# A two-layer decoder trunk on one core: masked decays, paired squares, block steps in a triangular inverse, queries spread by DMA, and four reorderings

## What is computed

```
# gated delta, per head, in chunks of c tokens
decay  = exp(where(causal, b[:, None] - b[None, :], -inf))
attn   = (q @ k.T) * decay
a      = strict_lower((k_beta @ k.T) * decay)
sol    = triangular_solve(I + a, [v * beta, k_beta * exp(b)])
o      = rms_norm(o_delta, norm_w) * silu(z)          # root mean square over 256 values of a head
# cross-attention of the samples, per sample and head
s      = q_sample @ mem_k.T * HD_X ** -0.5            # 256 memory rows, 256 values per head
# merge
merged = g0 * (o_ret @ w_ret) + g1 * (o_gdn @ w_gdn) + g2 * (o_mem @ w_mem)
```

## Time and profile before

| what | value |
|---|---|
| median of 3 runs | 1855.25 us (1853.64 to 1856.99) |
| the profiled execution, its own time | 1852.71 us |
| its span, first to last instruction | 1850.9 us |
| mean granted TensorE clock | 0.999 |
| busy: PE, DVE, ACT, POOL | 1803.7, 1321.4, 890.8, 118.8 us |
| DMA | 368.20 MB, mean 199 GB/s |

### The profile page before, as it was taken

The page is one execution under the profiler, slowest core; times in us unless marked ns, Lnnn a source line. Parts: engine busy times, 40 slices in busy tenths (PEclk is TensorE's granted clock), DMA queues, the critical chain, the costliest instruction groups (busy, mean ns, idle before and its releaser), DMA issues.

```text
span 1850.9 us, 40385 instructions
## 1 busy us (share of the span) xinstructions
PE 1803.7 (97%) x16247; PEld 1744.1 (94%) x16247; DVE 1321.4 (71%) x2077; ACT 890.8 (48%) x1044; POOL 118.8 (6%) x174
## 2 busy tenths in 40 slices
PE   6999999999999999999999999999999899999998
PEld 6999999988988999999999999998889799989998
DVE  6677577787777867777567765768777776877764
ACT  5443364546574254543364434454566434354433
POOL 0000001111210100000000000010112010000000
PEclk9999999999999999999999999999999999999999
DMA  7776667766864656666667766676778465556654
GB/s 232 218 207 191 180 198 225 235 227 211 284 227 137 198 160 226 170 191 168 173 200 219 206 185 201 195 243 206 236 242 267 144 201 171 169 148 186 182 164 133
DMA packets 433619, 368.20 MB, mean 199 GB/s; under 512 B 9395, under 2 KB 411125, under 8 KB 432811
## 3 DMA queue, kind: packets, MB, share of 16 engines
q1 hardware_dynamic: 409560, 276.60, 50.2%
q0 software_dynamic: 23872, 89.03, 14.3%
HBM read 338.90 MB, written 26.69 MB: 198 GB/s over the span
## 4 chain that ended last, share of the span: by engine, by line
PE 76%; DVE 14%; issue 5%; ACT 2%; DMA 2%; DVEq 0%; SPq 0%; ACTq 0%
PE proj L687 49%; PE proj L710 4%; PE proj L705 4%; PE proj L706 4%; DVE wl L1870 3%; PE proj L661 2%; PE aux L752 1%; PE aux L922 1%; ACT wh L1371 1%; PE aux L1144 1%; DMA raw<-w_mem_v 1%; PE aux L867 1%; PE aux L883 1%; DMA raw<-w_branch_gdn 1%; PE aux L1017 1%
## 5 line engine op out<-in xcount | busy, mean ns | idle before, releaser
L1870 DVE TENSOR_TENSOR wl<-raw,wh 128x2048 fp32r<-128x2048 f32 (+1 forms) x280 | 599.2, 2140 | 196.4 <-ACT wh L1371 172.6
L1371 ACT CAST wh<-raw 128x2048 fp32r<-128x2048 f32 (+1 forms) x280 | 500.3, 1787 | 245.0 <-PE proj L687 94.2
L687 PE MATMUL proj<-xh,wh 128*128 128x264 f32 x2624 | 379.6, 287 | 2.2 <-issue 2.2
L687 PE MATMUL proj<-xl,wh 128*128 128x264 f32 x2624 | 380.6, 285 | 0.0
L687 PE MATMUL proj<-xh,wl 128*128 128x264 f32 x2624 | 370.9, 284 | 0.1
L687 PEld LDWEIGHTS proj<-xl,wh 128*128 128x128 f32 x2624 | 341.3, 188 | 12.5 <-issue 12.3
L687 PEld LDWEIGHTS proj<-xh,wh 128*128 128x128 f32 x2624 | 340.1, 188 | 4.8 <-issue 3.0
L687 PEld LDWEIGHTS proj<-xh,wl 128*128 128x128 f32 x2624 | 338.9, 188 | 0.7 <-DVE wl L1870 0.6
L706 PE MATMUL proj<-hl,wh 128*128 128x264 f32 x704 | 173.3, 283 | 0.0
L705 PE MATMUL proj<-hh,wh 128*128 128x264 f32 x704 | 173.0, 283 | 0.0
L1392 ACT ACTIVATE gate<-gate 128x264 f32<-128x264 f32 x88 | 37.4, 425 | 242.1 <-DVEq L1905 242.0
(11 more groups left out here) (472 smaller groups left out, 2235.4 us busy)
## 6 DMA issues: line engine op xcount, KB each, us to landing
raw<-ffn_w_in SPq DMA_DIRECT2D x176, 512.0 KB, 5.2
raw<-w_in SPq DMA_DIRECT2D x80, 1024.0 KB, 5.6
raw<-ffn_w_out SPq DMA_DIRECT2D x64, 704.0 KB, 4.6
sring<-cache_mem_k POOLq DMA_DIRECT2D x32, 512.0 KB, 4.9
sring<-cache_mem_v POOLq DMA_DIRECT2D x32, 512.0 KB, 3.9
out<-sring POOLq DMA_DIRECT2D x32, 512.0 KB, 4.5
sring<-state_gdn POOLq DMA_DIRECT2D x30, 512.0 KB, 4.9
raw<-w_mem_v SPq DMA_DIRECT2D x8, 1024.0 KB, 6.2
```

Source lines behind the costliest of these rows:

```text
L687: mm = pe.matmul(o, w[:, s, k * 256 + t * P:k * 256 + (t + 1) * P], a[:, k, :], **go)
L1371: act.copy(wh[:, slot, 0:size], raw[:, slot, 0:size]).then_inc(hi_done[slot], 1)
L1870: dve.tensor_sub(wl[:, slot, 0:size], raw[:, slot, 0:size], wh[:, slot, 0:size].bitcast(F32)).then_inc(split_done[slot], 1)
```

## The change

Values that are computed stay the same. Seven edits:

1. The future half of a decay is set by the minimum: in place of 0 the minimum is taken with `future`, 0 in the triangle and -10000 outside, so both multiplications by `tri` go, and L2437 takes the decay itself as its last factor; L2441 and L2416 go.
2. DVE adds the squares of the two halves of a head (`pair_sums(sqd)`, in gz after the remainder of group 2), and `gm` has four products in place of eight.
3. The levels of groups 4 and 5 of the inverse work on blocks with tile positions: 16 and 24 products of 32 x 32 x 32 (`pair_blocks`, `pair_corrections`), then 8 and 8 of 64 x 64 x 64 (`half_blocks`, `half_corrections`). `gw`, `c_t` and `t_m` go. The second half of the last `gu` of the small levels moves from the end of group 3 into group 4.
4. Queries: DVE copies the row in float32 to `qrow`, POOL stores it to a tensor in DRAM, waits for the landing, and loads two rows at a time to all 128 partitions (`spread`, 256 KB, three buffers `qsp`). PE's `spread` goes. Of the 16 scores a layer, three stand in mq, where five stood.
5. `smt` moves one sixth of a group later; `rkn` is turned three products later, and DVE's `kn` is made in conv tile 1 of group 0, ahead of the remainder for group 2, where it stood in group 1. `mpt0` starts at bank 2.
6. `gdt` goes to bank 2 and `gkS` to bank 1; in x0 group 0 DVE stacks the keys (releases `gkS`) ahead of `sample_outputs`.
7. At the end of rg `gated(1)`, `gated_low` and `tell("o_ret")` stand ahead of `query_part(1)` and of the remainder.

```diff
-QUERIES = ["mkt0", "mqs0", "mkt1", "sp0", "gaw", "mqs1", "sp1", "gab", "sp2", "mqs2", "sp3", "sp4"]
+QUERIES = ["mkt0", "mqs0", "mkt1", "gaw", "mqs1", "gab", "mqs2"]
 STEPS = (["n1", "q1", "p1", "n2", "q2"] + QUERIES
-         + ["mqs3", "sp5", "ms0", "sp6", "ms1", "sp7", "mpt0", "sp8", "sp9", "mpt1", "sp10", "sp11",
-            "mo0", "sp12", "sp13", "mo1", "sp14", "sp15", "smt", "spt"]
+         + ["mqs3", "ms0", "ms1", "mpt0", "mpt1", "mo0", "mo1", "smt", "spt"]
...
+FIRST_BANK = {**{f"{n}{g}": b for g in range(LEVELS) for n, b in (("gc", 3), ("gu", 0))}, "gdt": 2, "gkS": 1, "mpt0": 2, "smt": 0, "gkn": 1, "gus": 1, "gmt": 3,
...
+        future = masks[:, 4, :]
...
+            def store_query(l, h):
+
+                pool.wait_ge(M["mqs"], l * H + h + 1)
+                passed(pool)
+                pool.dma_start(queries[l, h], qrow[:, h % 2, :]).then_inc(query_stored, 16)
+                pool.wait_ge(query_stored, 16 * (l * H + h + 1))
+
+            def spread(l, n):
+
+                h, b = n // 4, 2 * (n % 4)
+                if n >= 3:
+                    pool.wait_ge(unit_used[(n - 3) % SRING], l * (NUNIT // SRING) + (n - 3) // SRING + 2)
+                passed(pool)
+                pool.dma_start(qsp[n % 3][:], queries[l, h, b:b + 2].rearrange("b d -> (b d)").partition_broadcast(P)).then_inc(unit_loaded[n % SRING], 16)
...
+                store_query(l, 0)
+                for n in range(3):
+                    spread(l, n)
...
-                for n in range(SRING, V_UNIT):
-                    unit(l, n)
+                for n in range(2 * NS):
+                    if n in (0, 1, 3):
+                        store_query(l, (n + 1) // 2 + 1)
+                    if n + SRING < V_UNIT:
+                        unit(l, n + SRING)
+                    if n + 3 < 2 * NS:
+                        spread(l, n + 3)
...
-                def spread(n):
-
-                    h, b = n // 4, 2 * (n % 4)
-                    if b == 0:
-                        pe.wait_ge(M["mqs"], l * H + h + 1)
-                    o = begin(l, f"sp{n}")
-                    for z in range(2):
-                        mm = pe.matmul(o[:, 0, z * 256:(z + 1) * 256], selr[0:ROWS, b + z:b + z + 1].broadcast_to([ROWS, P]),
-                                       qst[:, h * 256:(h + 1) * 256], start=True, stop=True)
-                    end(mm, f"sp{n}")
-
...
+                def rest_inner(g, t, k):
+
+                    if g == 2 and (t, k) == (1, 1):
                         ready("sall")
                         turn(l, "smt", [(m * P, sall[:, m, :]) for m in range(2)])
-                    else:
-                        ready("spr")
-                        turn(l, "spt", [(m * 32, ps[:, m * P:(m + 1) * P]) for m in range(2)])
-
-                def rest(g):
-                    if g < 2:
-                        spread(13 + 2 * g)
-                products(l, "rv", xh, xl, after=rest, mid=rest_middle)
+
+                products(l, "rv", xh, xl, mid=rest_middle, inner=rest_inner)
...
+                    if g == 1 and (t, k) == (1, 0):
+                        ready("rot")
+                        turn(l, "rkn", [((2 * h + t) * P, rot[:, 4 + h, t * P:(t + 1) * P]) for h in range(H) for t in range(2)])
...
+                def pair_blocks(o):
+
+                    for n in range(8):
+                        for i in (0, 2 * BLK):
+                            first, second = slice(i, i + BLK), slice(i + BLK, i + 2 * BLK)
+                            mm = pe.matmul(o[second, n * BLK:(n + 1) * BLK], a_t[n // 4][first, n % 4, second], blk_t[first, 1, n, :],
+                                           start=True, stop=True, tile_position=(i, i + BLK))
+                    return mm
+
+                def pair_corrections(o):
+
+                    for n in range(8):
+                        c = slice(n * BLK, (n + 1) * BLK)
+                        for i in (0, 2 * BLK):
+                            second = slice(i + BLK, i + 2 * BLK)
+                            pe.matmul(o[i:i + BLK, c], blk_y[second, n, :], blk_t[second, 0, n, :], start=True, stop=True, tile_position=(i + BLK, i))
+                        mm = pe.matmul(o[BLK:2 * BLK, c], blk_t[BLK:2 * BLK, 0, n, :], blk_y[BLK:2 * BLK, n, :],
+                                       start=True, stop=True, tile_position=(BLK, BLK))
+                    return mm
+
+                def half_blocks(o):
+
+                    for n in range(8):
+                        mm = pe.matmul(o[HALF_P:P, n * HALF_P:(n + 1) * HALF_P], a_t[n // 4][0:HALF_P, n % 4, HALF_P:P], t_h[0:HALF_P, n, :],
+                                       start=True, stop=True, tile_position=(0, HALF_P))
+                    return mm
+
+                def half_corrections(o):
+
+                    for n in range(8):
+                        mm = pe.matmul(o[0:HALF_P, n * HALF_P:(n + 1) * HALF_P], y_h[HALF_P:P, n, :], t_t[n // 4][HALF_P:P, n % 4, HALF_P:P],
+                                       start=True, stop=True, tile_position=(HALF_P, 0))
+                    return mm
...
                     if g < SMALL and (t, k) == (1, 4):
                         corrections(g, 0)
-                    elif 0 < g < SMALL and (t, k) == (0, 1):
+                    elif 0 < g <= SMALL and (t, k) == (0, 1):
                         corrections(g - 1, 1)
-                    if g == SMALL + 1 and t == 0 and k in (4, 6):
-                        s = (k - 4) // 2
-                        pe.wait_ge(inv_t, l * 9 + 7 + s + 1)
-                        turn(l, f"gw{s}", [(q * P, t_t[s][:, q, :]) for q in range(4)])
+                    elif g == SMALL and (t, k) == (1, 4):
+                        pe.wait_ge(inv_y, l * 6 + 5)
+                        o = begin(l, f"gu{g}")
+                        end(pair_corrections(o[:, 0, :]), f"gu{g}")
+                    elif g == SMALL + 1 and (t, k) == (1, 4):
+                        pe.wait_ge(inv_y, l * 6 + 6)
+                        pe.wait_ge(inv_t, l * 8 + 7)
+                        o = begin(l, f"gu{g}")
+                        end(half_corrections(o[:, 0, :]), f"gu{g}")
...
-                        for s in range(2):
-                            if g > SMALL:
-                                pe.wait_ge(inv_m, l * 2 + s + 1)
-                            else:
-                                pe.wait_ge(inv_t, l * 9 + 5 + s + 1)
-                            o = begin(l, f"gy{g}{s}")
-                            for q in range(4):
-                                mm = pe.matmul(o[:, 0, q * P:(q + 1) * P], c_t[s][:, q, :], t_m[s][:, q, :], start=True, stop=True)
-                            end(mm, f"gy{g}{s}")
+                        pe.wait_ge(inv_t, l * 8 + g + 1)
+                        o = begin(l, f"gc{g}")
+                        end(pair_blocks(o[:, 0, :]) if g == SMALL else half_blocks(o[:, 0, :]), f"gc{g}")
...
-                    if g == SMALL - 1:
-                        corrections(g, 1)
-                    elif SMALL <= g < LEVELS:
-                        for s in range(2):
-                            pe.wait_ge(inv_y, l * 8 + 4 + 2 * (g - 4) + s + 1)
-                            o = begin(l, f"gt{g}{s}")
-                            for q in range(4):
-                                mm = pe.matmul(o[:, 0, q * P:(q + 1) * P], y_m[s][:, q, :], t_t[s][:, q, :], start=True, stop=True)
-                            end(mm, f"gt{g}{s}")
-                    elif g == 6:
+                    if g == 6:
                         ready("gvnd")
+                        pe.wait_ge(inv_t, l * 8 + 8)
                         per_head("gv0", lambda h: t_t[h // 2][:, 2 * (h % 2), :], lambda h: vn[:, 0, h * DV:(h + 1) * DV])
...
-                        ready("g2sq")
+                        second("g2sq", 1)
                         for s in range(2):
                             o = begin(l, f"gm{s}")
                             for hd in range(2):
-                                for dt in range(2):
-                                    mm = pe.matmul(o[:, hd, 0:SEQ], ones[:], sqd[:, 4 * s + 2 * hd + dt, :],
-                                                   start=(dt == 0), stop=(dt == 1))
+                                mm = pe.matmul(o[:, hd, 0:SEQ], ones[:], sqd[:, 2 * s + hd, :], start=True, stop=True)
...
-                    order(tt(y_m[s][:], y_m[s][:], tri[:].unsqueeze(1).broadcast_to([P, 4, P]), ALU.mult))
...
-                        order.apart(ts_(y_m[s][:, q, :], o[:, 0, q * P:(q + 1) * P], bc[:, col:col + 1], 0.0, ALU.subtract, ALU.min))
+                        order.apart(stt(y_m[s][:, q, :], o[:, 0, q * P:(q + 1) * P], bc[:, col:col + 1], future, ALU.subtract, ALU.min))
...
                     o = take(dve, l, f"gG{s}")[:, 0, :].rearrange("p (q m) -> p q m", q=4)
+                    second("dme", s)
                     for q in range(4):
```

(76 more changed lines are left out.)

118 lines of the change are left out of this document (47 added, 71 removed).

## The result

The changed kernel took 1833.0 us (median of 4 runs, 1829.6 to 1836.5), the kernel before 1854.5 beside it: ratio 0.988, 95% interval 0.9863 to 0.9896. That is 21.4 us faster, where 28.6 were forecast, and 6.4 above the 1826.6 predicted. The profiled execution took 1834.7 us with a span of 1832.9, so the two profiles differ by 18.0 us. That is 3.4 less than the medians do: the profiled execution of the kernel before was one of its quicker ones, that of the changed kernel one of its slower ones.

What follows compares the result with a forecast made beforehand. PE bounds the kernel, busy 1803.7 of 1850.9 us. Terms 4.2 + 4.6 + 4.4 + 1.1 = 14.3 us a layer, 28.6 in both, take 1852.7 to 1824.1; with 2.5 for the median, 1826.6, range 1820 to 1833 (chance 0.61).

Steps and rivals of the forecast that it cites:

- Spreads and turns: Query spreads taken off PE (3.6 us) and moved turns (0.6): 4.2 us a layer gained, bounds 2.5 and 5.
- The first query is told about a group and a half ahead of its score: Query spreads: later spreads also get 1.5 groups, 8.7 us, against a landing taken as 6 us; nothing charged.
- 5.2 us of cover: DVE's remainder behind the scores ends at 313.9, PE uses it at 319.07; late scores were charged nothing.
- a chain that the missing spread does not shorten: Between `ms1` and `mpt0`, through DVE and ACT: PE already waits 0.62 us there, so one spread gains nothing.
- My sign of being wrong: DVE's scores waiting several us for `sring` or `qsp`, then PE for `wl`; small sets above 2 us; x0 waits moved.
- Rival 3: Queries' way through DRAM: slower if a spread needs over 8.7 us to land; 1865 at 12.5 us; chance 0.05.
- `kn`, part of the same term: Moved turns in gq: `smt`, `rkn` and `kn` gain 0.4, 0.4 and 0.8, PE waits 1.0; net 0.6 us a layer.
- Start of x0: Four PE waits, 5.05 us together, go and up to 0.5 comes back: 4.6 us a layer, bounds 2.5 and 5.
- Rival 1: Waits come back elsewhere, DVE and remainders setting the pace in x0: 1835, range 1833 to 1841; chance 0.17.
- Inverse: Large levels: 7.9 us of PE replaced by sets of 3.3, less 0.2 for DVE: 4.4 us a layer gained.
- Rival 2: Small inverse products cost PE as much as full ones: 4.8 us a layer lost, 1845; chance 0.07.
- Paired squares: Squares at `gm`: 16 instructions of 3.62 us halve, less a wait of 0.5: 1.1 us a layer, bounds 0.3 and 1.7.

Runs made afterwards that it cites:

- k: The changed kernel with only the 1 MB store of `mkn` moved behind spread 5, POOL still waiting in line for each query's store; 1838.5 us, ratio 0.9913.
- c: The changed kernel with the turn `rkn` and the decayed keys `kn` back in their old place, behind group 1 of gq; 1833.4 us, ratio 0.9886.
- e: The changed kernel with query stores early and waited for late, `mkn` behind spread 5, and `rkn` and `kn` in their old place; 1828.8 us, ratio 0.9859.
- f: The changed kernel with each query's store issued early and waited for only ahead of its spread, `mkn` unmoved; run twice, 1827.9 and 1825.2 us.
- h: The changed kernel with the edits at the start of x0 undone, the inverse still in blocks; 1840.5 us, ratio 0.9923.
- i: The changed kernel with 16 products of squares again, without `pair_sums(sqd)`; 1837.2 us, ratio 0.990.
- b: The changed kernel with query stores issued early and waited for only ahead of their spreads, and the `mkn` store moved behind spread 5; 1828.7 us, ratio 0.9863.
- Kernel a: The changed kernel with queries spread by 32 TensorE products a layer again, all other edits kept; 1832.8 us, ratio 0.9886.

## Why the prediction was off by 6 us

**Spreads and turns, 4.2 a layer.** This is where it failed; the cuts measured -1.3 in layer 0 and -2.3 in layer 1, where some 1.4 more lie in the row ahead of `ms0`. Three readings in the step were wrong. "The first query is told about a group and a half ahead of its score" and "at 6 us some score may wait for a microsecond or two" took one landing as the price. POOL runs two in series, and a third where the next query's store comes between; the landings themselves were near what I took (4.5 for the first store, a median of 6.8 for the spreads). I had written that "POOL waits for each store", and still counted nothing for it. "5.2 us of cover" looked at the wrong client: PE never waited for that `wl`. The score stands ahead of `largest(1)` too, and that chain had no slack at all, since PE already waited 0.62 at its end. And "a chain that the missing spread does not shorten" is right, but the change could lengthen it. On top came the clock, 1.4 and 1.6 us. My sign of being wrong had the first half of this, waits of the scores of several us, and looked for the second at `wl` instead of at `mpt0`. "Beside weight loads that have the same cover" was wrong too: ACT waited 21.6 us for `w_in`. Rival 3, the way through DRAM, was the right mechanism in a smaller size, but it priced the landing of a spread alone. Of the 32 spreads four passed its 8.7 us (8.9 to 10.1), and their scores waited 0.3 to 2.0 us; score 4, which did the harm, had a spread of 6.1 and two stores in line ahead of it.

The Trainium skill ("DMA: Bandwidth & Descriptors", Queues, rings and completion order) says, in its paragraph on the queues of SP and ACT, that the semaphore increment of a DMA lands only after every earlier write of the same DMA engine. The traces agree for POOL's queue: an 8 KB store landed after 4.5 us alone and after 8.9 to 9.7 behind 1 MB, in the changed kernel and in k, each time 0.2 us behind the 1 MB. That it was this rule and not the queue's order that held the store back, no run here shows.

**`kn`, part of the same term.** Net 0.6 forecast, nothing that could be told from noise (c and e). The wait for `wl` was charged with 1.0 and is 0.89. In f `rkn` keeps 0.29 of its wait and `sv1` has a new one of 0.37.

**Start of x0, 4.6.** Measured 3.5 to 4.0 by h. The four waits went as described. PE now waits 0.54 for `go0` later in x0 and 0.25 for a `wl` in gz: DVE has less to spare, the small part of rival 1 that came true. The first is 0.47 in h, so it does not come from the start of x0. PE stops once a layer, for 1.31 and 1.50 us, at an instruction for which the profile names no releaser; before it had such stops of 0.91 and 1.27 nearby, and their cause is open. In h no such stop in x0 is above 0.19. So in layer 0 the stop of 1.31 can be most of what lies between the 4.78 us of waits that went and the 3.5 measured.

**Inverse, 4.4.** Right: 4.4 and 3.9. The sets were taken at 0.5, 0.8, 1.0 and 1.0 and took 0.62, 0.63, 1.07 and 1.07. The wait of 0.82 that I kept is gone. Rival 2 is out, and so is what the Trainium skill ("TensorEngine Tiling (Array Packing)", Gotcha 1: PSUM Pressure) would have made of it: 32 instructions (16 products) from two row positions into one bank took 0.62 us, 19 ns each, against 113 ns for a full-size one.

**Paired squares, 1.1.** The stretch at `gm` went from 3.27 us to 1.65 behind a wait of 0.33: 1.3.

Rival 1 named 1835, which is near the time measured, by another way: it expected the loss in x0, where only a seventh of it was (1.5 of 10.6). So the direction and three of the four terms came out by the mechanism that was forecast. But 1833.0 lies at the very edge of my own 1820 to 1833, and the room above it, up to 1841, was there for a rival that hardly happened. That the time stayed within 1818 to 1841 is in that part luck.

## What to carry to other kernels

When a product is replaced by a store and a load, the price is the whole line of the issuing engine: landings in series, whatever large transfer stands ahead, and each request queued behind the wait. Issue the store as soon as its data is there, and wait for it only ahead of its reader; that alone was worth 5 to 8 us here, in two sessions. And look for cover at the chain that already makes the bottleneck wait, not at the first client behind the late instruction: a chain with a wait of 0.6 us at its end has none.

## What was not expected of the hardware

Some waits of TensorE cost more than their length, because the granted clock fell behind them to 0.5, the lower of its two levels, for 3.4 us. In the changed kernel this happened behind the waits of 2.35 and 2.32 us and cost 1.4 and 1.6 us more. The length of a wait does not tell when it happens. In the profiles here, the end of the program aside, it fell at or within 1.5 us behind a wait of 1.55 us (c, at 1446.08), of 1.84 (i, at 1229.68), of 1.94 (k, at 1227.41), and at all those of 2.07 to 3.57 except one; it stayed at 1.00 at waits of 1.96 (the changed kernel, at 48.70), 2.05 (k, at 322.13) and 2.85 (b, at 49.34). In b and i it fell at two waits of 1.08 and 0.61 us with little between them. What decides is not shown here.

It goes with part of the scatter: the four runs of the changed kernel have mean clocks of 0.997, 0.996, 1.0 and 0.999 and took 1834.7, 1836.5, 1829.6 and 1831.3 us. Kernel a took 1833.5 us at 1.0 and 1832.2 at 0.999, so it is not all of it.
